# Moving eight query, key and value projections of linear attention into the mLSTM heads of a one-core decoder step

## The reference, cut to what matters

```
(gq, gk, gv, gr, ga, mq, mk, mv, mo, mi, mf, su, za, zb, zc) = split_in(hn @ w_in)
o_a = gla_chunked(gq * 64**-0.5, gk, gv, log_sigmoid(ga @ w_alpha + b) / 16)
y_a = head_rmsnorm(o_a) * silu(gr)
h_b = mlstm_chunked(mq * 128**-0.5, mk, mv, log_i, log_f)      # the matrix memory
y_b = head_rmsnorm(h_b) * sigmoid(mo)
y_c = gelu(s5(su)); y_c = y_c * sigmoid(y_c @ w_glu)
merged = sigmoid(za)*(y_a @ w_a) + sigmoid(zb)*(y_b @ w_b) + sigmoid(zc)*(y_c @ w_c)
```

## Time and profile before

| | us |
|---|---|
| median of three timed runs (2629.70 to 2634.02) | 2631.93 |
| the profiled execution, its own time | 2638.09 |
| its span in the trace | 2636.3 |
| PE busy | 2351.4 (89%) |
| DVE, ACT, POOL busy | 1149.7, 574.7, 268.0 |
| mean granted TensorE clock | 0.933 of full |

### The profile page before, as it was taken

One profiled execution on the slowest core, in us unless ns is written; L12 is line 12 of the kernel. 1 busy time (PEld: TensorE's weight loads), 2 busy tenths in 40 slices (PEclk: granted clock), 3 DMA queues, 4 the chain that ended last, 5 costly groups with the idle time before them and its releaser, 6 DMA issues.

```text
span 2636.3 us, 34651 instructions
## 1 busy us (share of the span) xinstructions
PE 2351.4 (89%) x14712; PEld 2249.5 (85%) x14712; DVE 1149.7 (44%) x1264; ACT 574.7 (22%) x716; POOL 268.0 (10%) x411
## 2 busy tenths in 40 slices
PE   5799977779985579999999999779999999999996
PEld 5699857568975469999999998669999999999995
DVE  4634413432236532122223432134665666666566
ACT  4422222221321122111212211232211111111112
POOL 6898300000000000000000000000000000000000
PEclk9899988878986669999999999989999999999997
DMA  6211113001210002121112124301111111111111
GB/s 226 87 50 49 49 67 104 17 34 34 80 40 5 16 5 77 48 80 48 47 42 104 48 72 161 135 9 48 52 47 49 48 49 41 49 49 48 41 49 68
DMA packets 35928, 156.35 MB, mean 59 GB/s; under 512 B 4176, under 2 KB 4240, under 8 KB 32336
## 3 DMA queue, kind: packets, MB, share of 16 engines
q1 hardware_dynamic: 27504, 100.22, 11.2%
q0 software_dynamic: 6864, 43.84, 4.3%
q10 hardware_dynamic: 1440, 10.49, 1.0%
HBM read 135.68 MB, written 19.02 MB: 59 GB/s over the span
## 4 chain that ended last, share of the span: by engine, by line
PE 81%; DVE 9%; ACT 5%; issue 3%; DMA 1%; POOL 1%; DVEq 0%; ACTq 0%; POOLq 0%
PE ps L249 21%; PE ps L250 21%; PE ps L252 21%; PE ps L1933 1%; DVE ATT L1565 1%; PE ps L989 1%; PE ps L359 1%; PE ps L360 1%; PE ps L362 1%; DVE CC L1228 1%; DMA scratch_yc<-YC 1%; ACT PA L2000 1%; PE ps L1308 1%; DVE GT L387 1%; PE ps L1609 1%
## 5 line engine op out<-in xcount | busy, mean ns | idle before, releaser
L249 PE MATMUL ps<-XH,WH 128*128 128x344 f32 x1608 | 520.7, 326 | 26.9 <-DVE WL L243 20.7
L250 PE MATMUL ps<-XL,WH 128*128 128x344 f32 x1464 | 469.7, 324 | 0.0
L249 PE MATMUL ps<-XN,WH 128*128 128x344 f32 x1248 | 396.6, 321 | 4.3 <-issue 4.1
L243 DVE TENSOR_TENSOR WL<-WRAW,WH 128x1024 fp32r<-128x1024 f32 x175 | 224.5, 1283 | 393.0 <-ACT WH L238 392.0
L250 PE MATMUL ps<-XN,WH 128*128 128x344 f32 x1248 | 394.7, 319 | 0.0
L252 PE MATMUL ps<-XH,WL 128*128 128x344 f32 x1608 | 345.0, 323 | 0.0
L249 PEld LDWEIGHTS ps<-XH,WH 128*128 128x128 f32 x1608 | 308.3, 192 | 30.9 <-issue 27.6
L238 ACT ACTIVATE WH<-WRAW 128x1024 fp32r<-128x1024 f32 x175 | 184.3, 1054 | 561.0 <-PE ps L252 545.0
L250 PEld LDWEIGHTS ps<-XL,WH 128*128 128x128 f32 x1464 | 280.7, 192 | 0.1
L252 PEld LDWEIGHTS ps<-XH,WL 128*128 128x128 f32 x1608 | 273.0, 191 | 0.0
L252 PE MATMUL ps<-XN,WL 128*128 128x344 f32 x1248 | 262.9, 319 | 0.0
(11 more groups left out here) (503 smaller groups left out, 3293.2 us busy)
## 6 DMA issues: line engine op xcount, KB each, us to landing
WRAW<-in_wslabs SPq DMA_DIRECT2D x175, 512.0 KB, 3.3
XIN<-in_xT POOLq DMA_DIRECT2D x1, 4128.0 KB, 18.4
scratch_mqk<-STAGE SPq DMA_DIRECT2D x8, 516.0 KB, 2.6
XR<-in_xT POOLq DMA_DIRECT2D x1, 4128.0 KB, 12.9
out_y<-XR SPq DMA_DIRECT2D x8, 516.0 KB, 3.0
CACHES<-in_ck ACTq DMA_DIRECT2D x4, 1024.0 KB, 14.3
CACHES<-in_cv ACTq DMA_DIRECT2D x4, 1024.0 KB, 11.9
CACHES<-in_ck POOLq DMA_DIRECT2D x3, 1024.0 KB, 15.7
```

Source lines behind the costliest of these rows:

```text
L243: nc.vector.tensor_tensor(WL[:, slot], WRAW[:, slot], WH[:, slot].bitcast(F32), ALU.subtract).then_inc(w_lo, 1)
L249: pe.matmul(out[t], WH[:, slot, w, :], xh(k, t), start=(k == 0), stop=False)
L250: pe.matmul(out[t], WH[:, slot, w, :], xl(k, t), start=False, stop=False)
```

## The change

1. Eight GLA groups (2 gq, 2 gk, 4 gv) leave the place after the mo groups. Their 64 k-steps are put into the four mLSTM heads, 16 for each head, at six points: 1, 4, 3, 3, 3 and 2 k-steps. Each group is copied to a staging tile, stored to HBM and loaded back by POOL after the last head. The slabs of mo move behind them.
2. To keep banks 0 to 2 for these groups, a head now uses banks 3 to 7 only, which adds waits (decay exponents wait for the copy of V, QK for KE, the second half of the chunk states for QA), and chunk states are 129 columns wide in place of 256.
3. `WPL`'s first two blocks, m0 and n0 are loaded sooner; `YC` is stored before the queries are loaded; the first DVE rows of mLSTM stand before the GLU, and ACT does its exponential and logarithm of them before it waits for the store of `YC`.
4. The GLA decay projection stands before the mo groups, its logarithms under them. As `ATT` and `VTOK` now lie over the mLSTM result, DVE and ACT begin GLA's own passes after the store to `scratch_yb`.
5. In S5, one k-step moves from point d to point c of each quarter.

```diff
-FILL = [(f"{q}{p}", k) for q in range(4) for p, k in
-        (("a", 3), ("b", 2), ("c", 2), ("d", 3), ("e", 2), ("f", 2), ("g", 2))]
+FILL = [(f"s{q}{p}", k) for q in range(4) for p, k in
+        (("a", 3), ("b", 2), ("c", 3), ("d", 2), ("e", 2), ("f", 2), ("g", 2))]
+FILL += [(f"m{h}{p}", k) for h in range(4) for p, k in
+         (("a", 1), ("b", 4), ("c", 3), ("d", 3), ("e", 3), ("f", 2))]
...
         def pool_mlstm(pool):
-            pool.wait_ge(yc_stored, 16)
-            pool.wait_ge(s5_stored, 16)
-            pool.dma_start(M0[:, :], I["m0"]).then_inc(ml_in, 16)
-            pool.dma_start(NS[:, :, :], I["n0"]).then_inc(ml_in, 16)
...
+            pool.wait_ge(fl_stored, 16 * 16)
+            pool.wait_ge(ml_dve, ml_did("qn", 4))
+            pool.dma_start(GVT[:, :, :], I["spill"][12:16].rearrange("h p n -> p h n")).then_inc(gl_in, 16)
...
         def act_mlstm(act, st):
-            act.wait_ge(yc_stored, 16)
             act.wait_ge(ml_x, 1)
             st.link(nc.scalar.activation(R[3][:, :], R[3][:, :], ACT.Exp, scale=-1.0))
             nc.scalar.activation(R[3][:, :], R[3][:, :], ACT.Ln, bias=1.0).then_inc(ml_l1, 1)
+            act.wait_ge(yc_stored, 16)
             act_project(act, SL_MV, G_MV, 2, MK, 4)
...
+                pe.wait_ge(ml_exp, NCH * (h + 1))
+                for k in range(2):
+                    last = pe.matmul(ps[:, 3 + k, :], spread(64 + h), ROWS[:, 512 * k:512 * k + 512], start=True, stop=True)
                 last.then_inc(ml_pe, 1)
                 pe.wait_ge(ml_dve, ml_did("st", h + 1))
+                for c in range(4):
+                    last = pe.matmul(grown(c), KE[:, c, :], V1[:, c, :], start=True, stop=True)
+                last.then_inc(ml_pe, 1)
+                pe.wait_ge(ml_dve, ml_did("qa", h + 1))
+                for c in range(4, 8):
+                    last = pe.matmul(grown(c), KE[:, c, :], V1[:, c, :], start=True, stop=True)
+                last.then_inc(ml_pe, 1)
+                pe_fill(pe, f"m{h}c")
...
+        def pe_gla_decay(pe):
+            pe.wait_ge(fl_free, 16)
+            pe.wait_ge(ml_on, 4)
             for hp in range(2):
                 for t in range(NTG):
                     last = pe.matmul(banks(hp)[t], WALPHA[:, hp * 128:hp * 128 + 128], GT[0:16, t * TG:(t + 1) * TG],
                                      start=True, stop=True)
                 last.then_inc(gl_a, 1)
+            pe_headnorm(pe, 0)
             pe.wait_ge(gl_x, 2)
-            pe_project(pe, SL_GQ, G_GQ, 2)
-            pe_project(pe, SL_GKV, G_GKV, 6)
-            evacuated(pe, G_GKV + 6)
+            pe_project(pe, SL_MO, G_MO, 4)
```

More of the change, by code:

```diff
@@ L217, in slab @@
                 sp.dma_start(WRAW[:, j % 2], I["wslabs"][j]).then_inc(w_loaded[j % 2], 16)
-            for j in range(SL_MQ + 4):
-                slab(j)
[L221 to L225, removed]
+            first = FILL_SLAB[-1] + 5
+            for j in range(first):
+                if j - 4 in FILL_SLAB:
+                    g = FILL_SLAB.index(j - 4)
+                    sp.wait_ge(fl_free, g + 1)
+                    sp.dma_start(I["spill"][g], staged(g)).then_inc(fl_stored, 16)
+                slab(j)
             assert (N_SLABS - first) % 2 == 0 and first % 2 == 1
@@ L1285, in pe_mlstm @@
                 for c in range(NCH):
-                    pe.transpose(two(0)[:, c, :], MVT[:, h, chunk(c)], IDENT)
-                    last = pe.transpose(two(2)[:, c, :], MKT[:, h, chunk(c)], IDENT)
+                    pe.transpose(two(3)[:, c, :], MVT[:, h, chunk(c)], IDENT)
+                    last = pe.transpose(two(5)[:, c, :], MKT[:, h, chunk(c)], IDENT)
                 last.then_inc(ml_pe, 1)
-                if h:
-                    pe.wait_ge(ml_dve, ml_did("qn", h))
-                for k in range(2):
-                    pe.matmul(ps[:, 4 + k, :], spread(h), ROWS[:, 512 * k:512 * k + 512], start=True, stop=False)
-                    pe.matmul(ps[:, 4 + k, :].rearrange("p (c i) -> p c i", i=128), IDENT,
-                              MASKNEG.unsqueeze(1).to_broadcast([128, 4, 128]), start=False, stop=True)
@@ L1295, in pe_mlstm @@
-                for c in range(NCH):
-                    last = pe.matmul(two(6)[:, c, :], MKT[:, h, chunk(c)], MQT[:, h, chunk(c)], start=True, stop=True)
-                last.then_inc(ml_pe, 1)
+                pe_fill(pe, f"m{h}a")
                 pe.wait_ge(ml_v, h + 1)
                 for k in range(2):
-                    last = pe.matmul(ps[:, k, :], spread(64 + h), ROWS[:, 512 * k:512 * k + 512], start=True, stop=True)
+                    pe.matmul(ps[:, 3 + k, :], spread(h), ROWS[:, 512 * k:512 * k + 512], start=True, stop=False)
+                    pe.matmul(ps[:, 3 + k, :].rearrange("p (c i) -> p c i", i=128), IDENT,
+                              MASKNEG.unsqueeze(1).to_broadcast([128, 4, 128]), start=False, stop=True)
@@ L1301, in pe_mlstm @@
+                pe.wait_ge(ml_dve, ml_did("ke", h + 1))
+                for c in range(NCH):
+                    last = pe.matmul(two(5)[:, c, :], MKT[:, h, chunk(c)], MQT[:, h, chunk(c)], start=True, stop=True)
                 last.then_inc(ml_pe, 1)
-                pe.wait_ge(ml_dve, ml_did("ke", h + 1))
                 for k, row in enumerate((0, 32, 96, 64)):
-                    last = pe.matmul(ps[:, 2, 8 * k:8 * k + 8], spread(row + h), ROWS[:, T:N], start=True, stop=True)
+                    last = pe.matmul(ps[:, 7, 8 * k:8 * k + 8], spread(row + h), ROWS[:, T:N], start=True, stop=True)
@@ L2306, in _ @@
             act_headnorm(act, 1, GVT)
-            gr_act(act)
+            for m in range(4):
+                gr_act(act, m)
             act_gates(act)
```

344 lines of the change are left out of this document (183 added, 161 removed).

## The result

The changed kernel takes **2552.1 us** (median of 4 runs, 2550.6 to 2552.5), the kernel before, timed beside it, 2633.0 (4 runs, 2629.7 to 2636.5): ratio 0.9692, 95% interval 0.9675 to 0.9708. It is 80.9 us faster, where 93.8 were forecast. The profiled execution took 2550.6 us of its own, with a span of 2548.5.

The account below looks back on a forecast made before the run. PE, busy 89% of the span, was taken as the bound, shortened only through its idle time or low clock. Terms summed to -93.8 us: profiled 2638.1 to 2544, carried to a median of 2538, range 2522 to 2574.

Parts of the forecast that it names:

- likeliest case: Whole kernel: the summed terms hold, 2538 us, own range 2528 to 2550, chance 0.73.
- S5: Stage S5: moving a k-step half covers each of four 1.2 us waits for the evacuation, -2.4 us.
- GLU start: Ahead of GLU: PE waits only for the gelu, no more for the `WPL` load, -7.6 us.
- value groups: mLSTM value groups: the 11.0 us idle goes, and the slow clock behind it, -14.0 us.
- heads: Four mLSTM heads: each takes 43.6 us with its 16 k-steps, 174.4 in place of 155.2, +19.2 us.
- eight groups, decay, mo: After the heads: eight GLA groups leave, -93.0 us; decay projection and mo groups at full clock, -5.0.
- entry to GLA: Start of GLA's passes: exposed store of the mLSTM result +8.0 us, plus 1 for slower clock behind it.
- 2.6 us more for each head: Heads: alternative estimate if transposes don't count as busy for the clock gate, 2548 us in place of 2538.
- the 1 us more for the clock: Entry to GLA: slower clock behind the gap left by the exposed store, 1 us.
- the profiled execution's 6.2 us: Whole kernel: profiled execution before, 2638.1, lies 6.2 above the timed median 2631.9; the difference was carried over to the forecast.
- More than forecast: Rival: shorter waits than forecast, above all at the entry to GLA, 2524 to 2530 us, chance 0.05.
- Slower: Rival: k-steps between short steps keep PE at 1.2 GHz through all heads, 170 us more, 2707, chance 0.03.

Follow-up runs that it names:

- lumped kernel: All 16 k-steps of a head put at its last point, f, against the changed kernel's spread over six points: 2613.6 us, ratio 0.9928.
- the shorter entry alone: Changed kernel with the mLSTM result stored in four parts, each when its head is done, in place of one store: 2547.6 us, ratio 0.9677.
- both gains: Changed kernel with the mLSTM result stored in four parts and TensorE's feed-forward loop written out: 2536.3 us, ratio 0.9630.

## Why the prediction was right, and where it was short

The direction, the mechanism and the range of 2522 to 2574 held; the predicted 2538 was 14 us low, and 2552.1 lies 2 us outside the likeliest case's own range of 2528 to 2550. By its steps, each from the two profiled executions:

| step | forecast | measured | from |
|---|---|---|---|
| S5 | -2.4 | -4.6 | end of S5 345.70 before, 338.27 after, less 2.9 that lies ahead of S5 |
| GLU start | -7.6 | -7.6 | idle 15.03, now 7.48 |
| value groups | -14.0 | -13.8 | lead 15.0 at GLU, 28.8 at the heads |
| heads | +19.2 | +20.7 | 155.2, now 176.0 |
| eight groups, decay, mo | -98.0 | -93.9 | lead 8.0 at the heads' end, 101.9 at mo's end |
| entry to GLA | +9.0 | +7.9 | lead 94.0 at PE's QT (766.95, now 672.94) |
| sum | -93.8 | -91.3 | |
| feed-forward loop | none | +7.9 | lead 96.4, then 88.5 |

These come from one pair of traces. The two kernels run again give S5 -3.3, GLU start -8.7, value groups -11.6, heads +18.9, eight groups, decay and mo -94.1, entry +7.9, in sum -90.9. The sum is firm and so are the last two terms; the others pass 1 to 2 us among each other.

**Heads.** 43.6 us for a head is what was worked out, 43.55 what is measured, the one uncovered wait (QA, forecast 0.6, measured 0.5) with it. The first head takes 45.2: its transposes are partly at half clock, and its first window shows 0.62. That is the 1.5 by which the term came out too large against the profiled execution before. But that execution had the shortest heads of three (155.2; 156.9 in the kernel before run again, 157.0 in the one with its loop written out), so that the total of this term owes something to the trace it was taken from; the 43.6 for a head does not. Part of the head's shortness is not hiding: the chunk states, 129 columns wide in place of 256, take 2.0 us (1.06, and 445.97 to 446.88) where they took 3.7. The forecast had this; no run changed it alone, and the lumped kernel has it too.

The Trainium skill, "TensorE: Matmul & The Clock Gate", section "PE-mode transpose", says that a transpose doesn't count as busy time of TensorE in the same way; by it the prediction had estimated 2.6 us more for each head. The granted clock of 1.00 with 24 transposes in each head decides against it here, in this mixture with matmuls. Transposes between matmuls cost no clock in these heads. The lumped kernel has the same transposes and 0.90: it is the waits and the place of the k-steps, not the transposes alone, that take the clock.

**Decay and mo, the term that was off.** I had put mo's four groups at full clock, 45.4 us. They take 48.4, from 608.68 to 657.07: the clock is 0.94 there, and was 0.96 before. From heads to mo it is 6.65, not 5.5; the decay projection, put at 3.4 us, takes some 1.5 more by its row. 4.1 us of the 5.0 didn't come. The windows show where the clock went (projection, then mo):

```profile
602.03:604.00 1.97, 1.97 (x8) 1.34 (x8) 1.67 (x4) 0.28 (x2) 0.00 (x0) 1.00 0.66 268
604.00:606.90 2.90, 2.90 (x7) 1.19 (x5) 1.23 (x1) 1.12 (x1) 2.35 (x4) 0.58 0.82 209
...
608.68:614.60 5.92, 5.92 (x22) 5.92 (x23) 2.09 (x7) 5.62 (x6) 0.00 (x0) 0.50 1.02 417
614.60:657.07 42.47, 42.47 (x269) 42.19 (x268) 19.87 (x33) 11.29 (x11) 0.00 (x0) 1.00 0.18 66
```

It fell to the lower level within the projection, with PE busy and before the wait of 1.33 us behind it, and the first 5.9 us of mo ran at half clock, which costs the 3.0 us by which mo is too long. The kernel before shows the same: there too the clock fell within the projection (1.00 from 660.34 to 663.00, 0.65 from 663.00 to 664.55). So the step that failed is the one that priced both the projection and mo at full clock. Why these twelve matmuls, which read 16 partitions and not 128, don't keep the clock, no run shows.

**Entry to GLA.** The exposed store took 8.1 us and the passes started 7.9 later than before: the +8.0 came as worked out, and the 1 us more for the clock didn't.

**The feed-forward loop** had no term. I took it that code the change doesn't touch keeps its time. It doesn't: TensorE's instructions ahead of it changed in number (the k-steps in the heads are written out, where the eight groups ran in a loop), and with it where the loop lies. This is 8 of the 14 us. That the larger part (4.9) hangs on the loop's place is shown by the padding by 48 and by 256 instructions and by the loop written out; the smaller (2.9, the pace) is only located.

**The rest.** The terms of the change came out 2.5 short. The end comes some 0.7 us later than TensorE's last matmul would have it: the last instruction of DVE ends 3.8 us before the end of the span in the kernel before and 4.5 in the changed one, with only the store of the output behind it, and so it is in the other traces of either layout; why isn't known. Carrying the profiled execution's 6.2 us over to the median held: 5.4 us of the lead, 2.9 ahead of S5 and 2.5 in GLA's passes, lie where nothing changed, and the kernel before, run again, has them too. What is then left is some 2 us, of which 1.5 is that the profiled execution of the changed kernel lies below its median (2550.6 and 2552.1). One sum of the prediction is off by 0.5 without effect: the GLU product from 353.1 ends at 384.0 by its row (30.86 us), not at 383.5.

**The rivals.** "More than forecast" (2524 to 2530, by a shorter entry to GLA) came in no kernel: the shorter entry alone gives 2547.6, and even both gains 2536.3. "Slower" is excluded at its root: the heads are at full clock.

## What to carry to other kernels

Cut work that waits for nothing into steps that are just longer than the hand-overs of the stage it is put into, and place them at the hand-overs: here the same steps in one lump were worth 61.5 us less. Count the clock that returns with the filled waits as part of the gain, and don't grant full clock to the first microseconds behind a gap or behind a projection like the decay's, which lost it while busy. After any edit of an engine's list, look at the "issue" stops behind the jumps back of its long loops: a loop of TensorE cost 0 to 2.5 us for each jump back, and writing it out, or a few dozen idle instructions ahead of it, gave 9 to 10 us back in the changed kernel; written out in the kernel before, it gave 2.6. A transfer in the way of the next stage goes out in parts, as its pieces are done.

## What the runs showed of the hardware that I had not expected

- 24 added transposes, 0.6 us of work, made the kernel 9.0 us faster, and 256 added instructions brought the stops back.
- A tiny transpose (4 by 4) costs 25 ns in a row of 128, though its row shows 161 ns from start to end.
- The clock fell to its lower level within the decay projection, with PE busy all the time, in both kernels.
- Two passes of the same matmuls, both with PE busy all the time and a clock of 1.00, differ by 0.6 us in 136, the same in every trace of one layout of tiles.
- Two executions of one kernel (2638.1 and 2629.8 us) differ by 3.2 us at one wait for weights near the start, which a comparison of two single traces inherits or not by chance.
